# Loading the last expert's gate and up ahead of the preceding down pieces, and one of its up pieces by 16 transfers of eight partitions

## The reference, cut to what matters

```python
g_idx = jnp.argmax(g_logits, axis=-1)                 # one group of 4 for each token
top_val, top_idx = lax.top_k(e_logits, EXPERT_TOPK)   # 2 of the group's 8 experts
gate = jax.nn.softmax(top_val, axis=-1) * g_w[:, None]
# for each expert e, over the tokens that chose it:
hid = jax.nn.silu(xblk @ w_gate[e]) * (xblk @ w_up[e])
out = hid @ w_down[e]
y = jnp.zeros((n_tok + 1, d), ht.dtype).at[tok_buf].add(out * w_buf[:, None])
```

## Time and profile before

| what | value |
|---|---|
| time, median of 3 executions | 1459.82 us (1459.47 to 1463.4) |
| profiled execution, its own time | 1460.15 us |
| its span | 1458.0 us |
| TensorE busy | 79% of the span |
| VectorE busy | 42% |
| ScalarE busy | 14% |
| mean granted TensorE clock | 0.914 |
| DMA, mean | 329 GB/s over 479.06 MB |
| DMA in slices 17 to 39 of 40 | 425 to 430 GB/s in each |
| DMA in the last slice | 261 GB/s |

### The profile page before, as it was taken

How to read it: one execution, slowest core, us unless ns; L and a number is a source line. 1 busy time by engine, 2 the same in 40 slices (tenths; PEclk the granted TensorE clock), 3 DMA queues, 4 the chain that set the end, 5 groups by cost and what they waited for, 6 DMA issues and landing times.

```text
span 1458.0 us, 19738 instructions
## 1 busy us (share of the span) xinstructions
PE 1149.9 (79%) x8515; PEld 590.7 (41%) x8515; DVE 611.1 (42%) x1281; ACT 209.8 (14%) x458; POOL 15.2 (1%) x31
## 2 busy tenths in 40 slices
PE   6999999999999899867664877667765776577666
PEld 5885564665884553322221322222222222222222
DVE  4889999678453443312221323112221222122312
ACT  4211012273012311100000100000000000000000
POOL 4000000000000000000000000000000000000000
PEclk9999999999999999988887988878888899888988
DMA  9443352612437679999999999999999999999996
GB/s 295 148 146 136 137 202 109 227 55 87 174 125 258 243 294 423 425 427 428 425 430 426 427 426 428 427 427 428 427 426 429 427 427 428 426 429 425 428 427 261
DMA packets 73526, 479.06 MB, mean 329 GB/s; under 512 B 14885, under 2 KB 21413, under 8 KB 45152
## 3 DMA queue, kind: packets, MB, share of 16 engines
q1 hardware_dynamic: 72176, 477.45, 79.8%
q0 software_dynamic: 864, 0.25, 0.1%
q10 hardware_dynamic: 400, 0.10, 0.0%
HBM read 475.67 MB, written 2.11 MB: 328 GB/s over the span
## 4 chain that ended last, share of the span: by engine, by line
PE 47%; DMA 44%; DVE 3%; ACT 3%; issue 1%; SPq 0%; DVEq 0%; ACTq 0%
DMA late_ring<-in_moe_w_up_dram 23%; DMA ring<-in_moe_w_up_dram 17%; PE bank L652 10%; PE bank L1163 8%; PE bank L673 6%; PE bank L943 5%; PE bank L1123 3%; DMA late_ring<-in_moe_w_down_dram 3%; PE bank L1210 2%; PE bank L1197 2%; PE bank L1053 2%; PE bank L934 2%; PE bank L636 1%; PE bank L1019 1%; ACT hT L1357 1%
## 5 line engine op out<-in xcount | busy, mean ns | idle before, releaser
L1163 PE MATMUL bank<-ring,x_gathered 128*32 128x256 f32 x2432 | 289.9, 433 | 126.4 <-DMA late_ring<-in_moe_w_up_dram 86.4
L2429 DVE TENSOR_TENSOR tokens_out<-tokens_out,bank 128x512 f32<-128x512 f32 x240 | 148.9, 682 | 440.0 <-PE bank L1210 440.0
L1163 PE MATMUL bank<-late_ring,x_gathered 128*32 128x256 f32 x1664 | 235.0, 433 | 84.8 <-DMA ring<-in_moe_w_up_dram 84.7
L1163 PEld LDWEIGHTS bank<-ring,x_gathered 128*32 128x32 f32 x2432 | 130.6, 122 | 240.3 <-issue 208.4
L1163 PEld LDWEIGHTS bank<-late_ring,x_gathered 128*32 128x32 f32 x1664 | 103.0, 122 | 156.5 <-issue 136.7
L652 PE MATMUL bank<-ring,hT 128*128 128x512 f32 (+2 forms) x416 | 156.3, 536 | 3.4 <-ACT hT L1357 2.6
L1123 PE MATMUL bank<-x_tok,select 128*32 128x512 f32 x512 | 115.8, 1032 | 6.4 <-DVE select L2330 3.2
L652 PEld LDWEIGHTS bank<-ring,hT 128*128 128x128 f32 x416 | 78.6, 190 | 78.5 <-issue 67.0
L2385 DVE TENSOR_TENSOR x_gathered<-bank,gain_cols 128x512 f32<-128x512 f32 x32 | 22.1, 692 | 185.7 <-PE bank L1148 185.7
L1654 ACT ACTIVATE x_slots<-bank 128x512 f32<-128x512 f32 x32 | 19.1, 597 | 475.9 <-PE bank L1123 475.9
L1210 PE MATMUL bank<-y_slots,weight_slots 32*128 32x512 f32 x496 | 82.1, 736 | 6.7 <-DVE tokens_out L2429 5.2
(11 more groups left out here) (431 smaller groups left out, 1106.5 us busy)
## 6 DMA issues: line engine op xcount, KB each, us to landing
ring<-in_moe_w_gate_dram SPq DMA_DIRECT2D x36, 2048.0 KB, 38.3
ring<-in_moe_w_up_dram SPq DMA_DIRECT2D x35, 2048.0 KB, 42.9
ring<-in_moe_w_down_dram SPq DMA_DIRECT2D x35, 2048.0 KB, 38.1
late_ring<-in_moe_w_up_dram SPq DMA_DIRECT2D x25, 2048.0 KB, 42.8
late_ring<-in_moe_w_gate_dram SPq DMA_DIRECT2D x24, 2048.0 KB, 38.4
late_ring<-in_moe_w_down_dram SPq DMA_DIRECT2D x23, 2048.0 KB, 38.5
ring<-in_w_in_dram SPq DMA_DIRECT2D x20, 1024.0 KB, 9.3
ring<-in_w_out_dram SPq DMA_DIRECT2D x16, 1024.0 KB, 5.6
```

The source lines that it names most:

```text
L1163: mm = pe.matmul(gu_bank[SLOTS * c:SLOTS * c + SLOTS, 0:256], XGT[:, at, k % 4, k // 4, :], pieces[c // 2][:, a:a + 256], start=k == 0, st ...
L2429: ins = v.tensor_tensor(y, x, mix[c][:, :], ALU.add)
```

## The change

**Order of loads.** `MAIN_LOADS` lists which piece is loaded as the g-th. Up to expert 20 it is the order of before. The last twelve are gate and up of 21, gate and up of 22, down of 21, down of 22. The places in the ring follow from g as before.

**One piece by rows.** The piece g = `BY_ROWS` = 133 is the last expert's second up piece (q = 3). It is loaded by 16 transfers in place of one: each takes 8 partitions that lie four apart (a, a + 4, ... a + 28 in one of four groups of 32 partitions). TensorE waits for all 16 (15 times 16 more on the semaphore).

**TensorE.** After the gate and up of expert 21 come the gate and up of 22 and the transposes of their sums (`turn_sums`), then down of 21, its two combines, the weight transposes of 22, and for each half h `last_down(h)` followed at once by `last_combine(h)`. `keep_token_columns` and its two banks are gone; all eight blocks at the end are added by VectorE, in the order of `LAST_BLOCKS`.

**ScalarE and VectorE** follow that order: ScalarE drains the sums of 22 ahead of the down result of 21 and the weights of 22; its two copies at the end are gone. VectorE makes the first product of expert 22 early, and the second once down of 21 has been computed (`hidden` is overwritten by it), then the additions of 21.

```diff
@@ -170,6 +170,9 @@
 HEAD_PIECES = PPE * MAIN
 HEAD_USES = [len([g for g in range(HEAD_PIECES) if SLOT_ORDER[g % MOE_RING] == i]) for i in range(MOE_RING)]
 MAIN_PIECES = PPE * (N_EXP - MAIN)
+LAST = N_EXP - MAIN - 1
+MAIN_LOADS = [(j, q) for j in range(LAST - 1) for q in range(PPE)]
+MAIN_LOADS += [(j, q) for qs in (range(4), range(4, PPE)) for j in (LAST - 1, LAST) for q in qs]
 FLOW = ("sel", "chosen_w", "x_rows", "x_rows_out", "x_cols", "x_cols_out", "pieces_done", "gu_out", "turned", "gate_th",
         "hid_part", "hid", "at_filled", "at_out", "y_out", "mixed", "added")
 
@@ -202,7 +205,7 @@
     "conv_y", "conv_th", "conv_z", "c_sq", "c_n", "qx_n", "xl_max", "xl_exp", "xl_p", "m_sq", "m_scale", "router_w", "g_parts",
     "g_exp", "choice", "columns", "tables", "sink_in", "sel", "chosen_w", "x_rows", "x_rows_out", "x_cols", "x_cols_out",
     "pieces_done", "gu_out", "turned", "gate_th", "hid_part", "hid", "at_filled", "at_out", "y_out", "mixed", "added",
-    "za_half", "wo_half", "wo_t", "wo_s", "wo_free", "wo_add", "row0_mixed", "over_part", "quarter_done", "last_down", "last_out", "last_mixed", "last_added", "last_copied", "stored",
+    "za_half", "wo_half", "wo_t", "wo_s", "wo_free", "wo_add", "row0_mixed", "over_part", "quarter_done", "last_down", "last_out", "last_mixed", "last_added", "stored",
 ]
 
 
@@ -445,9 +448,10 @@
             return per * b + more if isinstance(b, int) else b * per + (per * (FIRST - 1) + more)
 
 
+        LAST_BLOCKS = [(2 * h + c, tt) for h in range(2) for tt in range(TT) for c in range(2)]
+        BY_ROWS = MAIN_PIECES - 5
         last_rows = [rows_bank, turn_bank]
         last_y = [YS, XGS]
-        last_kept = [cols_bank, gu_bank]
 
         block = ctx.enter_context(nc.Block())
 
@@ -552,12 +556,17 @@
                 expert(g)
 
             def main_expert(g):
-                j, q, i = MAIN + g // PPE, g % PPE, MAIN_ORDER[g % MOE_RING]
+                j, q, i = MAIN + MAIN_LOADS[g][0], MAIN_LOADS[g][1], MAIN_ORDER[g % MOE_RING]
                 if j == N_EXP - 1 and q >= 4:
                     w = inp["moe_w_down"][0].rearrange("e (h p k) n -> p e h k n", p=P, k=2)
                     for h in range(2):
                         sp.dma_start(moe_slot(i)[:, PIECE * h:PIECE * h + PIECE].rearrange("p (k n) -> p k n", k=2),
                                      w[:, j, h, :, 1024 * (q - 4):1024 * (q - 4) + 1024]).then_inc(main_in[i], 16)
+                elif g == BY_ROWS:
+                    for r in range(0, P, 32):
+                        for a in range(r, r + 4):
+                            sp.dma_start(shape4(moe_slot(i)[a:r + 32:4, :], q),
+                                         moe_source(j, q)[a:r + 32:4, :, :]).then_inc(main_in[i], 16)
                 else:
                     sp.dma_start(shape4(moe_slot(i), q), moe_source(j, q)).then_inc(main_in[i], 16)
 
@@ -576,10 +585,8 @@
             for g in range(MOE_RING, MAIN_PIECES):
                 sp.wait_ge(main["pieces_done"], g - MOE_RING + 1)
                 main_expert(g)
-            for name, n, tt, c in (("last_added", 1, 0, 0), ("last_added", 2, 0, 1), ("last_added", 3, 1, 0),
-                                   ("last_added", 4, 1, 1), ("last_added", 5, 0, 2), ("last_copied", 1, 1, 2),
-                                   ("last_added", 6, 0, 3), ("last_copied", 2, 1, 3)):
-                sp.wait_ge(s[name], n)
+            for n, (c, tt) in enumerate(LAST_BLOCKS):
+                sp.wait_ge(s["last_added"], n + 1)
                 sp.dma_start(out[0, P * tt:P * tt + P, 512 * c:512 * c + 512],
                              Y[:, tt, 512 * c:512 * c + 512]).then_inc(s["stored"], 16)
             sp.wait_ge(s["stored"], 16 * TT * COLS)
@@ -1178,6 +1185,10 @@
             def turn_hidden(f, b):
 
                 pe.wait_ge(f["at_out"], tally(b, 1, 1))
+                turn_sums(f, b)
+
+            def turn_sums(f, b):
+
                 pe.wait_ge(f["gu_out"], tally(b, 1, 1))
                 for t in range(2):
                     mm = pe.transpose(turn_bank[:, P * t:P * t + P], GUS[:, :].rearrange("p (f t) -> p t f", t=2)[:, t, :], ident)
@@ -1224,23 +1235,19 @@
                                            w[:, 2 * half + k, 512 * c:512 * c + 512], start=k == 0, stop=k == 1)
                 mm.then_inc(s["last_down"], 1)
 
-            def keep_token_columns():
-
-                pe.wait_ge(main["added"], 2 * (N_EXP - MAIN - 1))
-                for c in range(2):
-                    pe.matmul(last_kept[c][:, :], ident, Y[:, 1, 512 * (2 + c):512 * (2 + c) + 512], start=True, stop=False)
-
             def last_combine(h):
 
                 pe.wait_ge(s["last_out"], h + 1)
+                if h == 0:
+                    pe.wait_ge(main["at_out"], LAST + 1)
                 for tt in range(TT):
-                    if h == 1 and tt == 0:
-                        pe.wait_ge(s["last_added"], 2)
+                    if h == 0:
+                        pe.wait_ge(main["added"], 2 * LAST)
+                    else:
+                        pe.wait_ge(s["last_added"], 2 * tt + 2)
                     for c in range(2):
                         r = slice(2 * SLOTS * c, 2 * SLOTS * c + 2 * SLOTS)
-                        kept = h == 1 and tt == 1
-                        b = last_kept[c] if kept else mix[TT * tt + c]
-                        pe.matmul(b[:, :], SWT[r, tt, :], last_y[h][r, :], start=not kept,
+                        pe.matmul(mix[TT * tt + c][:, :], SWT[r, tt, :], last_y[h][r, :], start=True,
                                   stop=True).then_inc(s["last_mixed"], 1)
 
             gather(head, 0, (1,))
@@ -1313,24 +1320,37 @@
 
             gather(main, 0)
             turn_rows(main, 0)
-            last = N_EXP - MAIN - 1
-            for j in range(last + 1):
-                place = [MAIN_ORDER[(PPE * j + q) % MOE_RING] for q in range(PPE)]
-
-                def arrived_main(slot, j=j, place=place):
+
+            def main_places(j):
+                return [MAIN_ORDER[MAIN_LOADS.index((j, q)) % MOE_RING] for q in range(PPE)]
+
+            def main_arrived(j):
+                place = main_places(j)
+
+                def arrived(slot):
                     if j == 0:
                         return wide_in[slot], n_reg * 16 + 16 * HEAD_USES[slot] + (16 if slot in SLOT_ORDER[:SPLIT] else 0)
-                    g = PPE * j + place.index(slot)
+                    g = MAIN_LOADS.index((j, place.index(slot)))
                     uses = len([a for a in range(PPE, g + 1) if a % MOE_RING == g % MOE_RING])
-                    return main_in[slot], 16 * uses + (16 if g >= MAIN_PIECES - 2 else 0)
-
-                straight(main, j, last, place, arrived_main)
-                if j < last:
-                    down(main, j, arrived_main, place[4:6])
-            keep_token_columns()
+                    return main_in[slot], 16 * (uses + (15 if g == BY_ROWS else g >= MAIN_PIECES - 2))
+                return arrived
+
+            for j in range(LAST):
+                straight(main, j, LAST, main_places(j), main_arrived(j))
+                if j < LAST - 1:
+                    down(main, j, main_arrived(j), main_places(j)[4:6])
+            place = main_places(LAST)
+            for i in range(4):
+                gate_up(main, LAST, i, LAST % 2, main_arrived(LAST), place[2 * (i // 2):2 * (i // 2) + 2])
+            pe.wait_ge(main["hid"], LAST)
+            turn_sums(main, LAST)
+            down(main, LAST - 1, main_arrived(LAST - 1), main_places(LAST - 1)[4:6])
+            for tt in range(TT):
+                combine(main, LAST - 1, tt)
+            pe.wait_ge(main["hid"], LAST + 1)
+            turn_weights(main, LAST)
             for h in range(2):
-                last_down(h, arrived_main, place[4 + h])
-            for h in range(2):
+                last_down(h, main_arrived(LAST), place[4 + h])
                 last_combine(h)
 
 
@@ -1655,10 +1675,18 @@
 
             def block_middle(f, b):
 
+                drain_weights(f, b)
+                act.wait_ge(f["pieces_done"], tally(b, PPE, 4))
+                drain_sums(f, b)
+
+            def drain_weights(f, b):
+
                 act.wait_ge(f["at_filled"], tally(b, 1, 1))
                 act.wait_ge(f["mixed"], tally(b, 2, 0))
                 nc.scalar.activation(flat(SWT[:, :, :]), turn_bank[:, 256:512], ACT.Copy).then_inc(f["at_out"], 1)
-                act.wait_ge(f["pieces_done"], tally(b, PPE, 4))
+
+            def drain_sums(f, b):
+
                 nc.scalar.activation(GUS[:, :], gu_bank[:, 0:256], ACT.Copy).then_inc(f["gu_out"], 1)
                 act.wait_ge(f["turned"], tally(b, 1, 1))
                 nc.scalar.activation(TH[:, :, :], gate_t, ACT.Tanh, scale=0.5).then_inc(f["gate_th"], 1)
@@ -1684,20 +1712,19 @@
                 block_end(head, i)
             act.wait_ge(head["mixed"], tally(n_reg, 2, 0))
             drain_rows(main, 0)
-            last = N_EXP - MAIN - 1
```

(39 more changed lines are left out.)

## The result

The changed kernel takes 1477.78 us in the median (1477.2 to 1482.36, 4 runs) where the kernel before takes 1461.61 in the same comparison (4 runs): a ratio of 1.0118, with a 95% interval of 1.0101 to 1.0136. By the ratio it is 17 us slower; the two medians lie 16.2 us apart. The forecast was 1465.5, 5.7 us above the kernel before, with a range up to 1469.5, so the sign was right and the size wrong by a factor of three.

What follows compares the result with a forecast made beforehand. The last loads' landings and the serial chain behind them bound the kernel. Landing at 1440.2 plus 23.5 gave an end at 1463.7, 5.7 us later: 1465.5 against the median; range 1455.5 to 1469.5, the forecast's own 1463 to 1468.

Steps and rivals of the forecast that it cites:

- piece -3: Third load from the end, now expert 21's second down piece: complete at 1435.3 with the reorder alone, 1440.2 by rows.
- L + 23.5: End of the span: 23.5 us of serial work after L, the landing of expert 21's second down piece; 22.7 before.
- Gate and up ahead cost nothing so long as the loads bind: TensorE: expert 22's gate and up done by about 1430; up to 10 us ahead of down 21 if uncovered.
- The step that failed: Piece by rows: double share on eight engines, late ones included, adds 5.7 us to the end; bounds on L -4.9 to +8.8.
- piece -6: Sixth load from the end, just ahead of the piece by rows: complete at 1420.5 on a late engine.
- the third, late engines and a shared way: Piece by rows: early engines' writes slow the double share's second half, 3.9 us more; L 1444.1, time 1469.4; chance 0.08.
- Late engines among the eight: Piece by rows: its eight engines include some finishing ten us behind the early ones, inferred from one transfer's 0.6 us straggler.
- rivals 1 and 2: Piece by rows on early engines: 1.1 us faster (0.20) or 1455.7 (0.10); with shared way into memory, 1463.6 (0.12).
- rival 4: Piece by rows: each of the 16 transfers takes other engines, load even; L 1435.3, time 1460.6; chance 0.05.
- The sign that was named for it: End of the loads: DMA share stays near 0.5 for longer than ten us if the forecast is right.
- The row read too lightly: DMA at 1438: share 0.50 and 201 GB/s, against 1.04 and 418 at 1432; used for the shared-way rival, chance 0.12.
- SP's queue: Load issue: 15 more issues at 0.43 us, 6.5 us, hidden by the 47.18 us from issue to landing; cost nothing.

Runs made afterwards that it cites:

- the order alone: The changed kernel with the last expert's second up piece loaded by one transfer again, new order of loads and work kept: 1462.99 us, ratio 1.0012 to the kernel before.

## Why the prediction was wrong, point by point

- *What bounds the kernel*: right. The loads' last landings bind, in the changed kernel too: piece -3 was complete at 1452.33, and TensorE took it up at 1452.37.
- *The order of loads and the chain, L + 23.5*: right. 23.1 from TensorE's start in the changed kernel, 23.2 with the order alone, which costs 1.8 us by its ratio where 0.8 was worked out. The combines, the additions and the second halves stand in the profile as they were added up. Two terms were off and nearly cancel, which is luck: the first half of the last down took 2.46 us and not 1.9, at a granted clock of 0.50 to begin with, and from the last addition to the end it was 2.9 us and not 3.8.
- *Gate and up ahead cost nothing so long as the loads bind*: this cover was gone. The text says that they are computed by about 1430, before the piece -3 "in any case below". They began their second half at 1442.98, since the piece by rows came so late, and stood on the path with 6.52 us. They added nothing to speak of, since piece -3 was complete at 1452.33, just as TensorE was through with the half before it. That the two met is luck.
- *The step that failed*: "So eight engines carry an 8-partition transfer, and the piece of 2 MB gives each of them 256 KB, 9.87 us, where it had 128 KB". Its first half holds, by the eight reports of each transfer. The 9.87 us are worked out at the full rate of an engine, and the rate of all loads fell to half in two valleys of 11 us. In reports: piece -6 was complete at 1426.42 in place of 1420.5, as the first valley held up all engines; the last row came 16.4 us behind it and not 9.87; from there to piece -3 it was 9.5, where 9.8 was worked out. So L became 1452.33 and not 1440.2. Against the kernel before, at 1435.3, this is 17 us, and the upper bound of that term was +8.8. The piece was treated as a question of how the load is shared out. The runs show that for the most part it is one of where the writes go: a piece in two transfers of 64 partitions, with no double share, lost as much (1.011), and the upper half alone by rows lost 0.7% over the order alone, the lower half nothing.
- *The rivals*: the third, late engines and a shared way (0.08), was nearest, but priced the way as one between few engines, 3.9 us, and put it at the second half of the piece alone for the late engines. In the profile the rate of everything halves, once for those that arrive early at the upper rows and once for those that arrive late; the two valleys begin 15 us apart where the engines stood 10 apart, since the first delays the second. The semaphore reports bear this out.
- *Late engines among the eight*: right, and a guess from one straggler. Two late ones are among them, so the condition of rivals 1 and 2 fails; rival 4 fails by the two early engines that had no rows. The sign that was named for it did not come: the DMA share at the end was to stay near 0.5 for over ten us, and from 1452 on it is 0.1 to 0.2, since three engines alone are behind.
- *The row read too lightly*: that the other half did not speed up when half the engines had stopped was taken to say that each engine is held by something of its own. It left out, as the runs suggest, the case in which the engines are laid so that they don't meet, and a transfer of another shape makes them meet.
- *SP's queue*: the 16 issues took 14.08 us, where 6.5 more than for one had been worked out, and the next down piece was issued at 1396.47. It did not bind: the engines were busy without a gap.
- *Which partitions, and why both valleys*: while rows went into partitions 64 to 127, and while transfers over 64 partitions ran, all loads together moved about 200 GB/s, half of the 425 of before; rows into 0 to 63 alone cost nothing, and the same rows into 64 to 127 cost 11 us more. The Trainium skill (SBUF — State Buffer, Door 1: The DMA port swizzle, and DMA: Bandwidth & Descriptors, The descriptor swizzle) gives 16 ports, eight for partitions 0 to 63 and eight for 64 to 127, and in a transfer over 128 partitions a port to each engine. By that, engines that all write one half of the partitions have half of the rate; the runs agree. That packets of all engines slowed down when only two of them still had rows is shown by the packets of 16 KB in the second valley (1.3 us from 1432 to 1438). The Trainium skill (DMA: Bandwidth & Descriptors, Back-pressure in remote DMA) says that a saturated port holds up engines that share the path to it, there of remote transfers; the valleys here fit that, but no run here shows a path or a port.

**Open.** Why the second valley is as deep as the first, though only two or three engines were still in the upper rows then, was not taken apart: it would need a transfer on one or two engines beside the stream, and none was tried. That writes to another engine's partitions are the cause is shown by where they go and where they don't cost; how they hold up the others is argued. Nor does the trace give engines names: the reports tell early from late, and no more.

## What to carry to other kernels

Where a stream of loads over 128 partitions keeps all 16 engines busy, as here at 425 GB/s, a transfer over fewer partitions in its midst can halve the rate of the whole stream while it lasts: split a tile by columns, with all 128 partitions in each part (1.0014 here), and not by partitions (1.011 here). Read the DMA share together with GB/s: busy engines with half the bytes were here a sign of engines in each other's way, half the share with half the bytes one of engines that had run out of work. And when a wait is shortened, see first what lands next: the move that took 2.5 us out from behind one wait won nothing that could be told until the work behind the next one was put in front of it.

## What the runs showed of the hardware that was not expected

- 16 DMA engines at a share of 0.84 to 1.11 moved 180 to 229 GB/s in the stretches shown while transfers over part of the partitions ran, and 401 to 442 before and behind. A packet of 16 KB took 1.26 to 1.3 us then, in place of 0.61.
- This holds while only two engines still have rows for partitions 64 to 127 (1432.9 to 1440.6 in the changed kernel).
- Eight transfers of eight partitions into 0 to 63 cost nothing (1.0003), the same into 64 to 127 cost 0.82%; exchanging the rows read did not help (1.0129).
- One such transfer has eight reports of landing. The 16 issues took 14.08 us, 0.88 each, where the issue of one piece just ahead took 0.33 to 0.43.
- Two transfers of 64 partitions cost 1.1%, two over 128 partitions of half the columns 0.14%, of which 0.12% are the order's.
